# Twenty products of the identity with itself on TensorE, ahead of the first gathered rows

## The reference

```
h = x + W_o [ norm(MLA(norm(x))) ; norm(FoX(norm(x))) ]   # two kinds of attention heads
h = h + CrossAttention(norm(h), norm(mem))                # 4 heads, 256 memory tokens
h = h + MoE(norm(h))                                      # 32 experts, top 4 of each token
out = norm(h)
```

## Time and profile before

| | us |
|---|---|
| median of 3 runs | 2810.28 (2808.55 to 2810.66) |
| profiled execution, its own time | 2811.26 |
| span of its trace | 2809.5 |
| TensorE busy | 2667.0 (95%) |
| VectorE busy | 1087.0 (39%) |
| ScalarE busy | 631.5 (22%) |
| GpSimd busy | 380.4 (14%) |
| mean granted clock of TensorE | 0.985 |

### The profile page before, as it was taken

How to read it: one execution, slowest core, us unless ns; L and a number is a source line. 1 busy time by engine, 2 the same in 40 slices (tenths; PEclk the granted TensorE clock), 3 DMA queues, 4 the chain that set the end, 5 groups by cost and what they waited for, 6 DMA issues and landing times.

```text
span 2809.5 us, 53205 instructions
## 1 busy us (share of the span) xinstructions
PE 2667.0 (95%) x19153; PEld 2279.7 (81%) x19154; DVE 1087.0 (39%) x2669; ACT 631.5 (22%) x1387; POOL 380.4 (14%) x394
## 2 busy tenths in 40 slices
PE   7999999888999999799999999999999999999994
PEld 5454456555477886799999999999999999999994
DVE  0111145553221223443333344444545445454543
ACT  0233344553011111011111111112121212212122
POOL 0000022221000000010111111111111111121112
PEclk9999999999999999899999999999999999999997
DMA  7111241123200001755666677777888888888873
GB/s 282 38 52 52 65 135 58 55 68 111 87 1 19 19 30 59 298 199 201 227 218 241 236 279 266 269 262 280 299 297 308 300 290 310 286 303 297 293 251 135
DMA packets 97191, 525.24 MB, mean 187 GB/s; under 512 B 23968, under 2 KB 46432, under 8 KB 72544
## 3 DMA queue, kind: packets, MB, share of 16 engines
q1 hardware_dynamic: 76352, 490.60, 47.5%
q0 software_dynamic: 20768, 33.65, 5.7%
HBM read 501.92 MB, written 56.85 MB: 199 GB/s over the span
## 4 chain that ended last, share of the span: by engine, by line
PE 90%; DVE 3%; issue 2%; ACT 2%; DMA 1%; POOLq 0%; DVEq 0%; ACTq 0%; POOL 0%; SPq 0%
PE bank L1188 45%; PE wide L1592 18%; PE wide L1188 9%; PE bank L1240 8%; PE bank L1181 5%; PE wide L1305 2%; PE bank L1556 2%; DVE biased L1816 1%; PE wide L1322 1%; PE bank L1361 1%; DVE prob_t L1827 1%; ACT prob L998 1%; DVE low L1807 0%; POOLq L717 0%; ACT sq_a L923 0%
## 5 line engine op out<-in xcount | busy, mean ns | idle before, releaser
L1188 PE MATMUL bank<-xe_t,slot 128*128 128x128 f32 (+4 forms) x8192 | 1024.0, 287 | 13.8 <-issue 12.7
L1188 PEld LDWEIGHTS bank<-xe_t,slot 128*128 128x128 f32 x8192 | 1014.6, 192 | 16.0 <-issue 15.9
L1592 PE MATMUL wide<-act_t,slot 128*128 128x128 f32 (+4 forms) x4096 | 513.2, 286 | 0.0
L1592 PEld LDWEIGHTS wide<-act_t,slot 128*128 128x128 f32 x4096 | 506.3, 191 | 0.0
L2092 DVE TENSOR_SCALAR glu<-bank,b_gu 128x256 f32<-128x256 f32 x256 | 123.9, 484 | 751.0 <-PE bank L1188 751.0
L1135 ACT ACTIVATE sig<-glu 128x256 f32<-128x256 f32 x256 | 106.7, 417 | 852.5 <-DVE glu L2092 850.1
L1240 PE MATMUL bank<-w_in,xt 128*128 128x512 f32 (+1 forms) x512 | 217.9, 579 | 3.8 <-DVEq L1735 3.8
L1144 ACT ACTIVATE y_t<-wide,b_dn 128x256 f32<-128x256 f32 x256 | 107.5, 471 | 434.5 <-PE wide L1592 434.5
L850 POOL DMA_INDIRECT xg<-d_xn,gidx x66 | 65.9, 999 | 903.6 <-DVEq L2051 893.5
L1240 PEld LDWEIGHTS bank<-w_in,xt 128*128 128x128 f32 x512 | 95.5, 191 | 103.6 <-issue 103.6
L863 POOL DMA_INDIRECT share<-d_gate,sidx x64 | 67.5, 1055 | 460.0 <-DVEq L2111 436.3
(11 more groups left out here) (272 smaller groups left out, 2308.5 us busy)
## 6 DMA issues: line engine op xcount, KB each, us to landing
slot<-in_w_gu SPq DMA_DIRECT2D x128, 2048.0 KB, 7.8
slot<-in_w_dn SPq DMA_DIRECT2D x64, 2048.0 KB, 7.7
w_in<-in_w_in SPq DMA_DIRECT2D x1, 6144.0 KB, 25.1
w_mem_k<-in_w_mem_kv SPq DMA_DIRECT2D x1, 4096.0 KB, 13.1
w_mem_v<-in_w_mem_kv SPq DMA_DIRECT2D x1, 4096.0 KB, 22.7
x_sb<-in_x SPq DMA_DIRECT2D x8, 512.0 KB, 3.3
cneg<-d_cneg SPq DMA_DIRECT2D x8, 512.0 KB, 6.8
w_o<-in_w_o SPq DMA_DIRECT2D x1, 4096.0 KB, 17.4
```

The source lines that it names most:

```text
L1188: m = pe.matmul(dst, l, r_, start=(k == 0), stop=(k == n - 1))
L1592: x = pe.matmul(pp2[b][:, (m % 2) * CAP:(m % 2) * CAP + w], slots[4 + m // 4][:, k, (m % 4) * P:(m % 4 + 1) * P], act_t[:, k, 0:w], start= ...
```

## The change

One line is added to TensorE's program, behind the reading of the bounds and ahead of the loops. Nothing reads what it writes, no semaphore is waited for or raised by it.

More of the change, by code:

```diff
@@ L1650, in _ @@
             below.append(E)
+            product(listed[:, 0:P], [(ident, ident)] * 20)
             at = pe.alloc_register("item_at")
```

## The result

The changed kernel takes 2816.24 us (median of 15 runs, 2813.29 to 2818.63), the kernel before 2810.28 in the same session (15 runs, 2808.52 to 2815.53). The ratio is 1.0018, with a 95% interval of 1.0010 to 1.0026: some 5 us slower, between 2.8 and 7.3 (the two medians alone differ by 6.0). The single runs of one kernel spread over 5 to 11 us in this case, so a few microseconds are told better from the traces than from the times, if each step is counted from the same event. That event is here the start of the index work (`e_index(0)`), at 1129.78 us before and at 1130.59 after; the 0.81 us between them arose ahead of the change. "+5.7" means 5.7 us behind it.

What follows compares the result with a forecast made beforehand. TensorE, busy 95% of the span, was taken as the bound. Delayed branch start 1135.5 + 5.1 branch + 2.45 to the transposes = 1143.05 against 1140.53: +2.5 us on the median 2810.28, so 2812.8 us; range 2809.2 to 2816.5.

Steps and rivals of the forecast that it cites:

- The array's time of the products: TensorE's array before the first transposes: 40 matmuls take 6.1 us, hidden by the sequencer's long branch and the gather.
- The sequencer's room: TensorE's sequencer leads the array by about 18 matmuls, so the long branch starts 4.1 us late, at about 1135.5.
- R3: Rival: TensorE's queue is 64 deep, delaying the branch only 1.7 us; +0.3 to +1.7, so 2811.3 us; chance 0.10.
- The jump: TensorE sequencer's branch over the empty width-256 class before the turn-in: 5.1 us when started later, bounds 3.7 and 6.5.
- The clock: TensorE's clock at the turn-in: falls back after the products, effect 0, bounds -1.1 and +1.7 us.
- R1: Rival: products keep TensorE's clock up at the turn-in and cost nothing, -1.1 us, 2809.2 us; chance 0.10.
- R2: Rival: before the turn-in, delay hidden by a shorter branch and earlier clock rise; about 2810.3 us; chance 0.15.
- R4: Rival: added instructions move the expert loops' code so it no longer fits; slower by over 0.2%, to 2917; chance 0.05.
- the late turn-in: First transposes after the sequencer's long branch start at 1143.05 instead of 1140.53: +2.5 us, bounds 0 and +4.5.

Runs made afterwards that it cites:

- the second trace: The changed kernel with twenty products run once more, on another chip in its own session, against the kernel before: +0.12% (0.03 to 0.21).
- the six reads: Kernel before plus six more reads of a bound by TensorE's sequencer, no products, against the kernel before: +0.11% (0.02 to 0.20).
- two and nine reads: Kernel before plus two or nine more sequencer reads of a bound, no products: two, one run, 2809.2 us; nine, +0.11% against before.

## Why the prediction was right

The path was right: the products are hidden as time of the array, the branch starts late by the room of the sequencer, and the turn-in stands behind the branch. Two sizes on it were off, the jump and the clock. By its own steps, in the order of the sum:

- *The array's time of the products.* 6.1 us were said; they took 6.25, and 7.5 in the second trace. Hidden, as was said. The rise of the clock, put at 3.5 us, came 3.2 us into them in the first trace and 5.9 in the second, so that the first fits so well is in part luck.
- *The sequencer's room.* 18 matmuls and a delay of 4.1 us: measured 4.0 (1136.3 less 1130.59, less the 1.7 of before) and 4.8. The three checks fit: 16 matmuls no delay, 40 narrow ones 4.7 (5.0), 80 of them 9.8 (8.6, by the same too early rise). R3, the queue of 64, would have started the branch at +3.4; no run shows it. That such a delay of the sequencer is enough for the loss is shown by the six reads on an idle array.
- *The jump.* 5.1 us were said between 3.7 and 6.5; it was 4.2 and 3.9. The term was too large by about 1 us: over the late jump the DMA share was 0.66, over the old one 0.86. The fetches of 1.9 and 1.0 us, read as a sign of the traffic, do not go with it: with 40 products, at a share of 0.97, the fetch took 1.0 us and the jump 6.7. The first transpose was therefore late by 1.6 us (2.2 in the second trace) and not by 2.5. That it was set by the sequencer and not by the gather is shown by taking the jump away: +9.5, at the landing.
- *The clock.* Zero was taken, with a bound of +1.7 for a lower stretch over the first expert. It came out as +2.2 (13.69 against 11.52) and +1.8. This is the step that failed. It is the largest part of the 3.4 us between 2812.8 and the measured 2816.2; the others are -0.9 from the jump, 0.1 inside the turn-in, 0.8 from ahead of the change, 0.2 further on, and 1.0 because the trace before lay 1.0 us above its median and the trace after lies on it. I read the fall of the clock before the turn-in rightly, and then assumed that it would rise again inside the turn-in as it did before. In the traces counted from the first transpose the rise came after 3.3 to 3.8 us (before, 8 and 40 products, two and nine reads) or after 8.0 to 9.3 us (20 products in both traces, 32 columns, six reads, no jump with none and with 20), and never between; where it had fallen in the middle of the turn-in, the second holds too. The kernel before happened to be of the first kind in its profile, and that it is so in every execution is not shown.
- *R1* failed by its own condition, the handing over of all 40 at once. Its gain exists: without the jump and with 32 products the turn-in ran at the upper clock and took 3.65 us up to the first gate product instead of 4.73. *R2* was half right on the jump (4.2 us), but 1.6 us stayed. *R4*: no new gaps at the experts, six pieces of "issue" as before.

The errors of the jump and the clock, -0.9 and +2.2, partly cancel: with 0.1 more inside the turn-in, +3.9 of the traces stand against +2.5 in the sum. The interval of the first session, 2.8 to 7.3, holds the +3.9 and not the +2.5; that of the second, 0.8 to 5.9, holds both. The move is 0.18%, just inside what I had called no change. That the range held is luck in good part: 2816.24 is 0.3 us below its upper end, which added a bound of 4.5 us for the late turn-in, where 1.6 came, to one of 1.7 us for the clock, where 2.2 came. And the first gate product stands at 1147.83 as foretold only because the stage began 0.8 us later in that run.

What stays open: why the times of the clock's changes, counted from the start of the index work, are so alike from one execution to another (the rise in the turn-in stands at +14.1 to +14.3 before, with 8 products and with two reads), and how often the kernel before is of the slower kind. Its single times lie in two groups in the first session (eleven from 2808.5 to 2811.2, four from 2813.9 to 2815.5), which would fit, but its trace was taken once. In the three later sessions its median was 2812.3 to 2813.4, and in the last one 12 of 27 runs lay above 2813. There the changed kernel costs less against it, +3.4 us. This points to a part of the clock that is smaller on average than the 2.2 us between the two traces; that is argued and not shown.

## What to carry to other kernels

Filler work on TensorE is free only if the sequencer has time to spare too: look at its rows in the hole, not only at the array's, for a branch over much code may be what ends the hole, and more matmuls than the room ahead of the array delay it. Fill up to the awaited event: a filler that ended 2 us early let the clock fall in the middle of the next work and gained nothing that can be told. The same piece of work can cost 2 us more or less by where it falls against the changes of the clock, so a small shift is to be judged from several runs and with the clock read in each trace.

## What the runs showed of the hardware

- About 18 float32 matmuls with their weight loads can stand ahead of TensorE's array; 16 were taken at once, 40 held the next branch back by 4.0 to 4.8 us. The Trainium skill gives the queue as 64 deep ("TensorE: Matmul & The Clock Gate", section "Architectural detail: the array is 16× 32×32, not 1× 128×128"); these runs show some 36 instructions.
- A branch over the code of one class took 3.8 to 6.7 us, the longer the more DMA traffic there was over it (share 0.45 to 0.97); the fetch of 16 KB within the jump of 6.7 us took 1.0 us. The Trainium skill ("Runtime: NRT & Kernel Launch", section "Instruction fetch mechanics") has the fetch that such a branch needs, and no time for it.
- The Trainium skill ("TensorE: Matmul & The Clock Gate", section "Part 4: PE-mode transpose") says that the full clock does not engage for transposes in transpose mode. The rows here name these transposes MATMUL and don't tell the mode. For them it is otherwise: the clock rose to 1.00 in the kernel before when nothing but transposes had run since 1131 us, and it stayed at 1.00 over them from 1139 to 1142 us, the second of the rows by stretches shown for 32 products.
